# First mixers of a two-block transformer: gates as half tangents straight from PSUM, log-gate functions over two places

## The reference, cut to what matters

```
def mixer(z, w_in, ...):
    h = z @ w_in
    (q_a, k_a, v_a, r_a, lr_f, lr_b, q_b, k_b, v_b, g_a, g_b) = jnp.split(h, SPLIT_POINTS, axis=-1)
    a = gla_branch(q_a, k_a, v_a, r_a, lr_f, lr_b, gla_w2, gla_b2, gla_gn)
    b = attention_branch(q_b, k_b, v_b, q_norm, k_norm, cos, sin)
    y = (jax.nn.sigmoid(g_a + b_merge[0]) * (a @ w_pa)
         + jax.nn.sigmoid(g_b + b_merge[1]) * (b @ w_pb))
    return y @ w_out
```

## Time and profile before

| | |
|---|---|
| median of 3 runs | 1918.5 us (1917.6 to 1921.14) |
| profiled execution | 1919.21 us, its span 1917.9 us |
| PE, PEld busy | 1878.0 us (98%), 1833.9 us (96%) |
| DVE busy | 1358.5 us (71%) |
| ACT busy | 1056.5 us (55%) |
| granted TensorE clock | 0.998 |
| DMA | 365.93 MB, mean 191 GB/s |

### The profile page before, as it was taken

The page is one execution under the profiler, slowest core; times in us unless marked ns, Lnnn a source line. Parts: engine busy times, 40 slices in busy tenths (PEclk is TensorE's granted clock), DMA queues, the critical chain, the costliest instruction groups (busy, mean ns, idle before and its releaser), DMA issues.

```text
span 1917.9 us, 36586 instructions
## 1 busy us (share of the span) xinstructions
PE 1878.0 (98%) x15273; PEld 1833.9 (96%) x15273; DVE 1358.5 (71%) x2401; ACT 1056.5 (55%) x1774; POOL 1.3 (0%) x8
## 2 busy tenths in 40 slices
PE   7999999999999999999999999999999999999998
PEld 6999998899999999999889999999999999999998
DVE  5777666577776677667558777688877558887744
ACT  6444565565444544455565544576566458656642
POOL 0000000000000000000000000000000000000000
PEclk9999999999999999999999999999999999999999
DMA  6776333346785577633235777444555554455553
GB/s 246 267 266 253 130 127 105 111 154 224 260 288 214 193 259 271 244 132 129 92 113 175 296 267 295 157 149 154 177 184 190 179 176 164 154 176 177 182 193 110
DMA packets 51812, 365.93 MB, mean 191 GB/s; under 512 B 6620, under 2 KB 8060, under 8 KB 9920
## 3 DMA queue, kind: packets, MB, share of 16 engines
q1 hardware_dynamic: 51648, 363.59, 54.0%
HBM read 362.52 MB, written 1.05 MB: 190 GB/s over the span
## 4 chain that ended last, share of the span: by engine, by line
PE 86%; DVE 6%; ACT 5%; issue 1%; DMA 1%; SPq 0%; DVEq 0%; ACTq 0%
PE bank L426 25%; PE bank L427 25%; PE bank L428 25%; DVE w_lo L1502 2%; PE bank L462 2%; PE bank L458 2%; PE bank L459 2%; ACT w_hi L1004 1%; PE bank L696 1%; PE bank L624 1%; DVE full L1544 1%; DMA raw_b<-in_weights 1%; PE bank L681 0%; DVE s_pool L1921 0%; PE bank L630 0%
## 5 line engine op out<-in xcount | busy, mean ns | idle before, releaser
L426 PE MATMUL bank<-xn_hi,w_hi 128*128 128x272 f32 (+2 forms) x2624 | 758.2, 289 | 1.2 <-DVE w_lo L1502 1.0
L428 PE MATMUL bank<-xn_lo,w_hi 128*128 128x272 f32 (+2 forms) x2624 | 748.4, 285 | 0.0
L427 PE MATMUL bank<-xn_hi,w_lo 128*128 128x272 f32 (+2 forms) x2624 | 748.0, 285 | 0.0
L426 PEld LDWEIGHTS bank<-xn_hi,w_hi 128*128 128x128 f32 x2624 | 494.4, 188 | 9.9 <-issue 6.3
L427 PEld LDWEIGHTS bank<-xn_hi,w_lo 128*128 128x128 f32 x2624 | 494.3, 188 | 1.1
L428 PEld LDWEIGHTS bank<-xn_lo,w_hi 128*128 128x128 f32 x2624 | 494.8, 189 | 0.0
L1502 DVE TENSOR_TENSOR w_lo<-raw_b,w_hi 128x1024 fp32r<-128x1024 f32 (+1 forms) x282 | 356.4, 1265 | 153.3 <-ACT w_hi L1004 152.6
L1502 DVE TENSOR_TENSOR w_lo<-raw_a,w_hi 128x1024 fp32r<-128x1024 f32 (+1 forms) x282 | 356.3, 1265 | 149.0 <-ACT w_hi L1004 148.5
L1004 ACT ACTIVATE w_hi<-raw_a 128x1024 fp32r<-128x1024 f32 (+1 forms) x282 | 306.9, 1090 | 251.1 <-PE bank L428 219.5
L1004 ACT ACTIVATE w_hi<-raw_b 128x1024 fp32r<-128x1024 f32 (+1 forms) x282 | 307.0, 1090 | 249.3 <-PE bank L428 227.0
L428 PE MATMUL bank<-h_lo,w_hi 128*128 128x272 f32 (+1 forms) x704 | 201.6, 286 | 0.0
(11 more groups left out here) (319 smaller groups left out, 2773.1 us busy)
## 6 DMA issues: line engine op xcount, KB each, us to landing
raw_a<-in_weights SPq DMA_DIRECT2D x123, 1024.0 KB, 4.8
raw_b<-in_weights SPq DMA_DIRECT2D x123, 1024.0 KB, 4.9
ada_raw<-in_ada_w SPq DMA_DIRECT2D x48, 1024.0 KB, 5.0
raw_a<-in_weights SPq DMA_DIRECT2D x16, 1408.0 KB, 5.8
raw_b<-in_weights SPq DMA_DIRECT2D x16, 1408.0 KB, 5.9
c_rows<-in_c_rows SPq DMA_DIRECT2D x3, 512.0 KB, 3.6
raw_a<-in_weights SPq DMA_DIRECT2D x2, 768.0 KB, 4.2
raw_b<-in_weights SPq DMA_DIRECT2D x2, 768.0 KB, 4.2
```

Of the source, the lines that this page charges most:

```text
L426: pe.matmul(o, wh, xh, start=start, stop=False)
L427: pe.matmul(o, wl, xh, start=False, stop=False)
L428: return pe.matmul(o, wh, xl, start=False, stop=stop)
```

## The change

1. `log_gates`: DVE's low part of `lrT` moves from place 4 to place 3; there it waits for both copies. The functions of the three products are cut after the second: two at place 4, the third at place 5, on ACT and DVE. PE turns values 0, 1 and 2 all at place 7, before it was 0 and 1 at place 6 and 2 at place 7.
2. r: ACT writes tanh(r/2) straight from the bank, DVE turns it to (tanh + 1) * r with a scalar_tensor_tensor that reads the bank; the gain of the norm is halved instead (`half`, two small DVE instructions at the mixer's start). The Silu at place 17 is gone. Set 0 is loaded at place 14, set 6 at place 19.
3. Merge gates: tiles 20 to 26 as before; at place 27 set 0 is loaded, tiles 27 to 33 are written as tanh straight from the bank, and tiles 0 to 8 are turned to tanh in place, two each at places 27 to 30 and one at 31. Both Sigmoids are gone. Merges become (g + 1) * bank, y's high part takes scale 0.5, y's low part becomes a scalar_tensor_tensor with 0.5. Set 6 is loaded at place 41.
4. Three small rope buffers move behind the raw buffer of the modulation weights.

```diff
@@ scalar_program, log_gates @@
             act.activation(la, la, ACT.Ln, bias=c.ones[0:n, 0:1]).then_inc(*k.up("gla_a", ("ln", l, t)))
+            if t == 1:
+                yield
...
@@ scalar_program, mixer @@
-                moved(u, c.r_act[:, at - 14, live], at % 2, ("in", l, at), cols=live)
-                if at == 17:
-                    act.wait_ge(*k.newest("tile_a"))
-                    act.activation(c.r_act[:, :, live], c.r_act[:, :, live], ACT.Silu).then_inc(*k.up("tile_a", ("silu_r", l)))
-                    load_table(LN_EXP_SET)
+                if at == 14:
+                    load_table(EXP_TANH_SET)
+                act.wait_ge(k.sem["unit_done"], u + 1)
+                act.activation(c.r_act[:, at - 14, live], bank[at % 2][:, live], ACT.Tanh, scale=0.5).then_inc(*k.up("tile_a", ("tanh_r", l, at - 14)))
+            elif at == 19:
+                load_table(LN_EXP_SET)
             elif 20 <= at < 34:
-                moved(u, c.gates[:, at - 18, live], at % 2, ("in", l, at), bias=c.v1[:, V_BM + at - 18:V_BM + at - 17], cols=live)
-                if at == 33:
...
-                    sigmoid(c.gates, 0, ("sig", l, 0), live)
-            elif at == 34:
-                sigmoid(c.gates, 8, ("sig", l, 1), live)
+                g = c.gates[:, at - 18, live]
+                if at < 27:
+                    moved(u, g, at % 2, ("in", l, at), bias=c.v1[:, V_BM + at - 18:V_BM + at - 17], cols=live)
+                else:
+                    if at == 27:
+                        load_table(EXP_TANH_SET)
...
+                    act.wait_ge(k.sem["unit_done"], u + 1)
+                    act.activation(g, bank[at % 2][:, live], ACT.Tanh, bias=c.half[:, at - 18:at - 17], scale=0.5).then_inc(
+                        *k.up("tile_a", ("in", l, at)))
+                    for m in range(2 * at - 54, min(2 * at - 52, 9)):
+                        g = c.gates[:, m, live]
+                        act.activation(g, g, ACT.Tanh, scale=0.5).then_inc(*k.up("tile_a"))
...
+            elif at == 41:
                 load_table(LN_EXP_SET)
@@ vector_program @@
         dve.memset(c.la[:, 0, :], 0.0).then_inc(*k.up("gla_v", ("clear", l)))
+        dve.wait_ge(*k.at("gla_a", ("lrT", l)))
+        dve.tensor_tensor(c.lrT[32:64, :], bank[4][0:32, 0:T], c.lrT[0:32, :].bitcast(F32), ALU.subtract).then_inc(*k.up("gla_v", ("lr_lo", l)))
         yield
-        dve.wait_ge(*k.at("gla_a", ("lr_hi", l)))
-        dve.tensor_tensor(c.lrT[32:64, :], bank[4][0:32, 0:T], c.lrT[0:32, :].bitcast(F32), ALU.subtract).then_inc(*k.up("gla_v", ("lr_lo", l)))
...
+        for j, first, n in ((0, V_BM, 16), (16, V_GN, 4)):
+            dve.tensor_scalar(c.half[:, j:j + n], c.v1[:, first:first + n], 0.5, None, ALU.mult).then_inc(*k.up("tile_v", ("half", l) if j else None))
...
+            if 14 <= at < 18:
+                r = c.r_act[:, at - 14, live]
+                dve.wait_ge(*k.at("tile_a", ("tanh_r", l, at - 14)))
+                dve.scalar_tensor_tensor(out=r, in0=r, scalar=1.0, in1=bank[at % 2][:, live], op0=ALU.add, op1=ALU.mult).then_inc(
+                    *k.up("tile_v", ("in", l, at)))
...
-                    dve.tensor_tensor(g, g, bank[b][:, live], ALU.mult).then_inc(*k.up("tile_v", ("merge", l, at, b)))
+                    dve.scalar_tensor_tensor(out=g, in0=g, scalar=1.0, in1=bank[b][:, live], op0=ALU.add, op1=ALU.mult).then_inc(
+                        *k.up("tile_v", ("merge", l, at, b)))
...
@@ tensor_program, mixer @@
-                for j in {6: (0, 1), 7: (2,)}.get(u, ()):
+                for j in (0, 1, 2) if u == 7 else ():
                     values_turned(l, j)
```

More of the change, by code:

```diff
@@ L197, in __init__ @@
         block_start = place
[L200 to L206, removed]
+        self.v1, self.bada, self.half = sb("v1", [P, V1_ALL]), sb("bada", [P, L, 48]), sb("half", [P, 20])
         self.att = [sb(f"att{i}", [P, T]) for i in range(4)]
@@ L211, in __init__ @@
         self.c_rows, self.ada_raw = sb("c_rows", [P, D]), sb("ada_raw", [P, 2 * D])
+        self.angle, self.turns, self.rest = (sb(n, [96, N]) for n in ("angle", "turns", "rest"))
+        self.posi = sb("posi", [96, N], I32)
         ffn_end = place
@@ L774, in mixer @@
                 tile(u0 + u, b, TA if u == 12 else live, c.xn_hi, c.xn_lo)
-                free[b] = [("tile_v" if u in (18, 19) else "tile_a", ("in", l, u))]
+                free[b] = [("tile_v" if 14 <= u < 20 else "tile_a", ("in", l, u))]
                 if u == 8:
@@ L1269, in moved @@
             act.activation(dst, bank[b][rows, cols], ACT.Identity, bias=bias).then_inc(*k.up("tile_a", key))
-    def sigmoid(gates, first, key, cols):
-        g = gates[:, first:first + 8, cols]
-        act.activation(g, g, ACT.Sigmoid).then_inc(*k.up("tile_a", key))
     def mixer(l):
@@ new lines, in mixer @@
+                act.wait_ge(k.sem["unit_done"], u + 1)
+                act.activation(c.r_act[:, at - 14, live], bank[at % 2][:, live], ACT.Tanh, scale=0.5).then_inc(*k.up("tile_a", ("tanh_r", l, at - 14)))
+            elif at == 19:
+                load_table(LN_EXP_SET)
+            elif 20 <= at < 34:
+                g = c.gates[:, at - 18, live]
[4 more added lines that the diff above has]
+                        load_table(EXP_TANH_SET)
+                        act.wait_ge(*k.at("tile_v", ("half", l)))
+                        act.wait_ge(*k.at("tile_v", ("in", l, 19)))
+                        act.wait_ge(*k.at("tile_a", ("in", l, 26)))
+                    act.wait_ge(k.sem["unit_done"], u + 1)
[4 more added lines that the diff above has]
+                        act.activation(g, g, ACT.Tanh, scale=0.5).then_inc(*k.up("tile_a"))
+                    if at == 33:
+                        k.value["tile_a", ("gate", l)] = k.count["tile_a"]
+            elif at == 41:
@@ L1326, in mixer @@
                     act.wait_ge(*k.at("tile_v", ("merged", l, m)))
-                    act.activation(c.y_hi[:, m, live], c.gates[:, m, live], ACT.Copy).then_inc(*k.up("x_hi", ("y", l, m)))
+                    act.activation(c.y_hi[:, m, live], c.gates[:, m, live], ACT.Copy, scale=0.5).then_inc(*k.up("x_hi", ("y", l, m)))
     def latent(l, name, n_k, width, src, hi):
@@ L1751, in gla @@
                 dve.tensor_tensor(f, bank[2 + h % 2][:, live], c.gate[:, 0, live], ALU.mult).then_inc(*k.up("gla_v", ("normed", l, h)))
-                dve.wait_ge(*k.at("tile_a", ("silu_r", l)))
+                dve.wait_ge(*k.at("tile_v", ("in", l, 14 + h)))
                 dve.wait_ge(*k.newest("gla_v"))
-                dve.scalar_tensor_tensor(out=f, in0=f, scalar=c.v1[:, V_GN + h:V_GN + h + 1], in1=c.r_act[:, h, live], op0=ALU.mult,
+                dve.scalar_tensor_tensor(out=f, in0=f, scalar=c.half[:, 16 + h:17 + h], in1=c.r_act[:, h, live], op0=ALU.mult,
                                          op1=ALU.mult).then_inc(*k.up("gla_v", ("gated", l, h)))
@@ L1832, in mixer @@
             finish(chains, at)
-            if at in (18, 19):
+            if 14 <= at < 18:
[3 more added lines that the diff above has]
+                    *k.up("tile_v", ("in", l, at)))
+            elif at in (18, 19):
                 j = at - 18
@@ L1838, in mixer @@
             elif 34 <= at < 38:
-                dve.wait_ge(*k.at("tile_a", ("sig", l, 0)))
+                dve.wait_ge(*k.at("tile_a", ("gate", l)))
                 dve.wait_ge(k.sem["unit_done"], u + 1)
@@ L1842, in mixer @@
                     g = c.gates[:, m, live]
-                    dve.tensor_tensor(g, g, bank[b][:, live], ALU.mult).then_inc(*k.up("tile_v", ("merge", l, at, b)))
+                    dve.scalar_tensor_tensor(out=g, in0=g, scalar=1.0, in1=bank[b][:, live], op0=ALU.add, op1=ALU.mult).then_inc(
+                        *k.up("tile_v", ("merge", l, at, b)))
             elif 38 <= at < 42:
-                dve.wait_ge(*k.at("tile_a", ("sig", l, 1)))
                 dve.wait_ge(k.sem["unit_done"], u + 1)
@@ L1865, in mixer @@
                 for m in (2 * at - 76, 2 * at - 75):
-                    low(c.y_lo[:, m, live], c.gates[:, m, live], c.y_hi[:, m, live], ("y", l, m))
+                    dve.wait_ge(*k.at("x_hi", ("y", l, m)))
+                    dve.scalar_tensor_tensor(out=c.y_lo[:, m, live], in0=c.gates[:, m, live], scalar=0.5, in1=c.y_hi[:, m, live].bitcast(F32),
+                                             op0=ALU.mult, op1=ALU.subtract).then_inc(*k.up("x_lo", ("y", l, m)))
     def latent(l, name, n_k, total, squares, src, hi, lo, gain):
```

2 lines of the change are left out of this document (removed).

## The result

The changed kernel takes 1907.8 us (median of 5 runs, 1906.65 to 1909.15) against 1918.5 (5 runs, 1917.5 to 1921.33): ratio 0.994, 95% interval 0.9929 to 0.9952. Direction and mechanism held; the size did not.

The account below looks back on a forecast made before the run. The prediction took PE, busy 98% of the span, as the bound, so only its idle time counted. It summed -2.9 - 3.4 - 2.2 + 0.8 = -7.7 us, from 1918.5 to 1910.8, range 1908.8 to 1914.4.

Parts of the forecast that it names:

- The wait of 1.4 goes: Log gates, place 4: PE no longer waits for the low part of `lrT` before the second product; 1.4 us gained.
- the 1.5 of `L743` go too: Places 6 and 7: PE's wait for the value tiles to be turned goes, 1.5 us, with 1.1 us of slack.
- -2.7 - 0.3 - 0.4: r, place 17: waits for `kend_t` (2.7 us), `pt` in mixer 1 (0.3) and the probabilities (0.4) all go.
- -0.9: Merge gates, mixer 0, places 33 and 34: `pt` copies no longer stand behind loads and Sigmoids; 0.9 us gained.
- -1.3: Merge gates, mixer 1: DVE's merges no longer wait for the second Sigmoid and weight parts behind it; 1.3 us gained.
- part 1: Log gates: PE's waits for the low part of `lrT` and for turned values both go; -2.9 us.
- part 2: r: the load, Silu, load block at place 17 goes and loads at 14 and 19 are covered; -3.4 us.
- part 3: Merge gates: -2.2 us from places 33 and 34, +0.8 us from late scores at place 28; -1.4 us.
- (b): Rival: the score at place 28 gets no cover in either mixer, 3.8 us in place of 0.8, 1913.8 us; chance 0.16.
- (b2): Rival: every table load holds ACT about 1.4 us longer than its row, 1913.6 to 1913.8 us; chance 0.03.
- (c): Rival: another wait behind a removed one voids one part, 1913.7 or 1914.2 us; chance 0.14, 0.10 for under 3.8 us gained.
- (d): Rival: slower, ACT becomes the bound at the new places of loads and tanhs, up to 1926 us; chance 0.05.

Follow-up runs that it names:

- Part 1 alone: The kernel before with only the log-gates change (low part a place sooner, functions over two places, values turned at place 7): 1917.2 us, ratio 0.9985.
- Part 3 alone: The changed kernel with the log gates and r as in the kernel before, so only the merge-gates change remains: 1918.1 us, ratio 0.9996.
- Second load at place 27: The changed kernel with another table load, of another set, ahead of the one at place 27: 1912.8 us in one execution.

## Why the prediction was wrong, point by point

**The step that failed** is the price of a removed wait: "The wait of 1.4 goes", "the 1.5 of `L743` go too", "-2.7 - 0.3 - 0.4", "-0.9", "-1.3". Each figure is the sum of a row of waits. Measured by start times:

| term | forecast | measured |
|---|---|---|
| part 1 | -2.9 | -3.6 (1.80 in each mixer) |
| part 2 | -3.4 | -4.8 (1.88 and 2.90) |
| part 3 | -1.4 | -1.9 (0.54 and 1.35) |
| sum | -7.7 | -10.3; whole mixers -10.27 |

Two things are missing in the rows. A wait row counts from the modelled end of the last matmul, 0.16 us after the point at which the next could have started: shown for the low part of the log gates, 0.71 against 0.87. The same is seen, smaller, in part 2 (1.21 to 1.28, 1.50 to 1.57, 0.28 to 0.35, 0.40 to 0.47). For the two kv products that is because they start 0.21 instead of 0.13 behind their forerunner also when nothing holds them; for the other two it was not worked out. At the merges of mixer 1 it is larger (0.18 and 1.13 by the rows, 0.41 and 1.35 by start times), since there the matmul behind the held one starts 0.08 late as well. And hand-overs that end before the modelled end of the matmul ahead give no row of PE. With the one `L624` row that the prediction left out they are 1.1 us of part 2 over both mixers, for which it had nothing.

**What is left between 10.3 and 10.7** is less than the interval of the ratio can tell, and the clock would be enough for it, which is not shown. At an equal mean clock of 0.998 the kernel before takes 1917.8 to 1918.2 in the seven such runs beside parts 1 to 3 and the changed one 1907.8 (one run), 10.0 to 10.4 apart, but the five such runs beside the later experiments spread from 1917.0 to 1919.2; the changed kernel's runs lie at 0.997 to 0.999, those of the kernel before at 0.996 to 0.998.

**Part 1.** Right: nothing behind the moved low part is late, the copy of value tile 2 (ACT, 247.79) is done 1 us before PE is through tile 7, as followed. That the move of the turning products counts for nothing was implied there but not said.

**Part 2.** Right that both loads are covered, now shown with two in place of one. Its price per instruction on DVE held: the new ones take 0.426 in the middle (0.415 taken). This row is from the forms of the changed kernel:

```profile
L1850 DVE SCALAR_TENSOR_TENSOR r_act<-r_act,bank x8: 412/426/439, 282.2 to 907.7; 128x272 f32<-128x272 f32 x4, 128x256 f32<-128x256 f32 x4
```

The prediction looked for what follows the removed block in mixer 1 alone, because only there wait rows stood.

**Part 3.** The new wait came with the forecast size, by another split. ACT in mixer 0 of the changed kernel:

```profile
353.62 1.28 ACT L990 ACT_TABLE_LOAD   x1
354.91 0.49 ACT L1316 ACTIVATE gates<-bank,half 128x272 f32<-128x272 f32 x1
355.30 0.74 ACT L1320 ACTIVATE gates<-gates 128x272 f32<-128x272 f32 x2
355.94 0.25 ACT L1236 ACTIVATE pt<-bank 16x128 f32<-16x128 f32 x1
```

The two tanhs take 355.30 to 355.94, 0.64 as taken. The score is only 0.16 late, and then the first turning product of place 29 0.07 and, inside that group, the one that needs the second probability tile 0.21, where "I get the probabilities 0.3 us before PE turns them" had nothing late: 0.44 in all, near the forecast 0.46. That the two agree is in part luck, for the score was forecast to take all of it. Mixer 1 lost 0.43 at the score (0.34 forecast). The lower bound given for the two, 0.5, was worked out for one tanh in place of two: 0.28 less overlap gives 0.2. The merges and y's low part take what they took:

```profile
L1863 DVE SCALAR_TENSOR_TENSOR gates<-gates,bank x16: 411/424/439, 382.5 to 997.0; 128x272 f32<-128x272 f32 x8, 128x256 f32<-128x256 f32 x8
...
L1888 DVE SCALAR_TENSOR_TENSOR y_lo<-gates,y_hi x16: 415/426/436, 399.6 to 1012.1; 128x272 fp32r<-128x272 f32 x8, 128x256 fp32r<-128x256 f32 x8
```

So no halving for two fp32 sources in SBUF, which the page Vector Engine (DVE) Microarchitecture Reference of the Trainium skill, section Points that are easy to get wrong, speaks of.

**The rivals.** (b), (b2), (c) and (d) did not happen. The range was built from them, from -0.8 for hidden scores and from the scatter of a median; it gave nothing for the possibility that a removed wait is worth more than its row. That is why it ended 1 us too high. The 0.10 of (c) for under 3.8 us gained is too much as well: without part 1 the gain is 4.8, without part 2 it is 4.3, and only without both does it fall below.

## What to carry to other kernels

Where matmuls follow each other, price a removed PE wait by start times: the start of the held matmul less the start of the one before it less their undisturbed distance, not by the idle time that a row of waits gives. Then look at the idle times of PEld, and for groups of the same products that take longer in one layer or place than in another, since waits shorter than a matmul's row leave no row of PE. And give the range room on the side of a larger gain as well.

A difference of a few microseconds in 1900 is read from stretches of two traces, aligned by the same instruction, with the granted clock beside them; the medians of part 1 and part 3 alone, 1.6 and 0.7 us below the kernel before, would have told a wrong story.

## What the runs showed of the hardware

The granted clock fell to its lower level for a few microseconds in the middle of a kernel whose PE is 98% busy, four times in the mixers of these traces, each time 1 to 2.5 us after a wait of PE had ended:

- Part 1 alone, mixer 0: 0.51 from 388.0 to 391.5, after 0.92 of waiting that ended at 385.6.
- Part 1 alone, mixer 1: 0.52 from 917 to 920, after 1.50 that ended at 915.5.
- Part 3 alone, mixer 1: 0.51 from 918.5 to 922, after 1.50 that ended at 917.6.
- Second load at place 27, mixer 1: 0.63 from 970 to 974, after 1.63 that ended at 967.4.

One such fall cost 1.5 to 1.6 us by start times. It does not always come: the profiled execution of the kernel before has the same 1.50 us wait without it, and the changed kernel keeps a wait of 1.6 for probabilities and had none. That a wait causes the fall was not tested by itself; that the changed kernel, with fewer long waits, runs at a slightly higher mean clock fits it.

At the start of an execution the matmuls are 0.23 us apart, as in the stretch of lower clock from 26.9 to 30.1 of the kernel before, though the windows give a granted clock of 1.00 there (10 to 16 us). So the start distance of PE's matmuls tells the speed where the column does not.
